# A hybrid conformer and HGRN2 block on one core: the first three chunks projected without the shift, which is added later

## The chip, the core and the metric

The kernel runs on one NeuronCore of a Trainium2 chip. Its engines are TensorE (PE, matrix products), VectorE (DVE), ScalarE (ACT), GpSimd (POOL) and SyncE (SP, which here only issues transfers). Each runs its own instructions in program order, and they wait for one another through semaphores. The metric is device time in microseconds (us) of one execution; lower is better.

## What is computed

The reference is one layer of a trunk with a sequence of 1024 tokens and a width of 1024. Only its head matters here:

```python
cond = jax.nn.silu(c)
mod = cond @ w_ada[l] + b_ada[l]
sh1, sc1, gt1, sh2, sc2, gt2 = [m[:, None, :] for m in jnp.split(mod, N_MOD, axis=-1)]
h = rms_norm(x, g_pre_mix[l]) * (1.0 + sc1) + sh1
zin = h @ w_in[l]
cv_val, cv_gate, q, f, i, og = jnp.split(zin, splits, axis=-1)
out_a = conformer_conv(cv_val, cv_gate, ...)   # u = val * sigmoid(gate), a causal convolution of 31 taps
out_b = hgrn2(q, f, i, og, lb_all[l], hgrn_norm_g[l])
...
```

`sc1` (the scale) and `sh1` (the shift) each take the product of `cond` with a 1024 x 1024 block of `w_ada`, 4 MB each. `w_in` is 1024 x 3072.

## The kernel before

Everything is float32. A product of two float32 matrices is made of three fp32r products: each operand is split into a high part (a copy rounded to fp32r) and a low part (the operand less its high part), and high x high, high x low and low x high are summed in PSUM.

The input projection is done in 24 chunks of 128 output columns, in five per head (`gate`, `val`, `i`, `f`, `q`) for four heads and then four `og` chunks. A chunk runs over 8 slices `kt` of the width, with 6 matmuls of 128x512 in each: 48 in all. Chunk g uses the PSUM pair g % 2, the weight slot g % 3 (`WS`) and the raw slot g % 2 (`RAW`). The normalised, scaled and shifted tokens, turned so that the width lies on the partitions, are `ha_hi`, `ha_lo` (kt 0 to 3) and `hb_hi`, `hb_lo` (kt 4 to 7).

**The prelude**, until the tokens are ready, works in 16 groups (`GROUPS`), each one kt and one half of the tokens. For a group PE turns four tiles of x (`turn_x`, L1989); ACT takes them out of PSUM with scale and shift at once (`full_and_high`, L994) and rounds them to the high part (L998); DVE subtracts for the low part (`low_half`, L1426), which counts `h_ready`; then PE projects the group for chunks 0 and 1 (`project_group`, L2004, six matmuls per group). Scale and shift come in four blocks of 256 columns: DVE sums 8 rows of a block, scale and shift side by side in 512 columns (`sum_rows`, L1400, L1403, L1408), PE sums over the partitions (`mod_sums`, L1976), and DVE adds the bias rows (`scale_shift`, L1415, L1417). A group cannot be turned before its block's numbers are there.

The order of work within an engine is written out by hand; nothing is scheduled by a planner. SP loads block 0, four tiles of x, the weights of chunks 0 and 1 (`load_chunk`, L541), the other four tiles of x, and blocks 1 to 3. POOL splits the weights of chunks 0 and 1 when they land, and those of chunk 2 only after `acc_ready` has reached 4, that is after DVE's last block; then it writes `masks_late` and clears `pmat`.

**The main part** is a loop over five periods of 40 pieces (a piece is one kt of one chunk; period 0 starts at piece 16, which is chunk 2). PE projects, and between projections runs small steps of the head before, called slots (`SLOTS`, `PLACES`). Slot `M` (L1953) sums the next rows of ada over the partitions; it waits until POOL has added all eight rows (`add_ada`, L756). The `S` slots are the levels of the recurrence, in which DVE does the work between. POOL's order in the first turns is: low parts of chunks 3 and 4 (`low`, L744), a row of ada, the low part of chunk 5, two rows, a late tap (L765), and so on to the rows 6 and 7. DVE does 54 steps of the convolution per head (`tap`, L1524), spread by `TAPS_FIRST` (how many of them in the head's own period) and the rest over the first 16 pieces of the next period; the first tap needs u = val * sigmoid(gate) (`gated`, L1510). `chunk_freed(1)`, for which chunk 3 waits, is the count of `gated`.

## Time and profile before

| | |
|---|---|
| time, median of 3 runs | 1127.62 us (1127.52 to 1127.94) |
| span of the profiled execution | 1124.7 us |
| between the span and the median | 2.9 us |
| PE busy | 1089.5 us, 97% of the span |
| DVE busy | 823.3 us, 73% |
| POOL busy | 751.2 us, 67% |
| ACT busy | 498.9 us, 44% |
| granted TensorE clock | 1.00 in the stretches looked at |

The profile holds one execution. Its page and the trace behind it give, for each instruction, when it ran and what ended the idle time before it. An instruction that is held up after it has been issued is shown as longer, not as waiting. The profiled execution's own time is not given apart from its span; the 2.9 us around the span are taken to stay as they are.

### The profile page before, as it was taken

The numbers are of one execution on the slowest core, as the hardware profiler recorded it, in microseconds if no ns is written. First come the engines' busy times: TensorE is split into PE (matmuls) and PEld (weight loads), VectorE is DVE, ScalarE is ACT, GpSimd is POOL, SyncE is SP. The second block draws the span as 40 slices with busy tenths as digits, with TensorE's granted clock in tenths as the row PEclk, the third lists the DMA queues.
The fourth block names the chain that finished last, engine by engine and source line by source line (L and its number), as shares of the span: only waits on it lengthen the run. The fifth ranks groups of instructions, "written<-read, shape, count | busy, mean of one in ns | idle before, by whom it ended". The sixth has DMA issues, their size and how long they took to land.

```text
span 1124.7 us, 14554 instructions
## 1 busy us (share of the span) xinstructions
PE 1089.5 (97%) x5140; PEld 907.7 (81%) x5140; DVE 823.3 (73%) x1168; ACT 498.9 (44%) x815; POOL 751.2 (67%) x645
## 2 busy tenths in 40 slices
PE   2899999999999999999999999999999999999996
PEld 1688888888888888888888888888888888888885
DVE  5977997979998755678775767666666666666658
ACT  5665575574652834345333323333333333233334
POOL 4179666675773640427977777868686969696966
PEclk9999999999999999999999999999999999999999
DMA  9644332333311271202322222222221222222217
GB/s 330 198 143 136 99 111 74 115 94 95 94 38 38 70 249 75 93 26 80 92 68 65 76 66 71 71 63 71 62 77 58 74 68 66 70 63 74 66 48 297
DMA packets 104745, 107.49 MB, mean 96 GB/s; under 512 B 6525, under 2 KB 84578, under 8 KB 104674
## 3 DMA queue, kind: packets, MB, share of 16 engines
q1 hardware_dynamic: 103216, 102.26, 29.0%
q10 hardware_dynamic: 1458, 4.31, 1.0%
q8 instruction: 41, 0.67, 0.3%
q14 instruction: 30, 0.25, 0.1%
HBM read 98.16 MB, written 8.40 MB: 95 GB/s over the span
## 4 chain that ended last, share of the span: by engine, by line
PE 94%; DVE 2%; ACT 1%; SPq 1%; issue 1%; DMA 1%; DVEq 0%; ACTq 0%
PE pair L2235 34%; PE pair L2041 23%; PE pair L2255 17%; PE pair L2144 8%; PE pair L2077 2%; PE pair L2198 2%; PE pair L2278 2%; PE pair L2004 1%; DMA x<-in_x 1%; DVE acc L1403 1%; PE pair L2072 1%; PE pair L2091 1%; PE pair L1965 1%; SPq L541 1%; PE pair L2093 1%
## 5 line engine op out<-in xcount | busy, mean ns | idle before, releaser
L1826 DVE TENSOR_TENSOR yt<-yt,pair 128x512 f32<-128x512 f32 x264 | 176.2, 684 | 34.6 <-PE pair L2255 34.6
L1524 DVE SCALAR_TENSOR_TENSOR pair<-u,conv_w_col,pair 128x512 f32<-128x512 f32 x208 | 139.6, 750 | 1.9 <-ACT pair L1120 1.4
L844 POOL TENSOR_TENSOR raw_r<-raw,w_hi 128x512 fp32r<-128x512 f32 x68 | 96.3, 1417 | 65.1 <-ACT w_hi L1256 65.1
L756 POOL TENSOR_TENSOR acc<-acc,ada 128x256 f32<-128x256 f32 x112 | 92.1, 854 | 55.9 <-ACT ada L1057 54.6
L2255 PE MATMUL pair<-w_hi,op_hi 128*128 128x512 f32 x280 | 109.2, 390 | 0.0
L2255 PE MATMUL pair<-w_hi,op_lo 128*128 128x512 f32 x280 | 109.0, 389 | 0.0
L2255 PE MATMUL pair<-w_lo,op_hi 128*128 128x512 f32 x280 | 108.9, 389 | 0.0
L853 POOL TENSOR_TENSOR w_lo<-w_lo_f,w_hi 128x512 fp32r<-128x512 f32 x70 | 95.1, 1359 | 0.0
L2235 PE MATMUL pair<-t_lo,w_hi 128*128 128x512 f32 x240 | 93.7, 390 | 0.0
L2235 PE MATMUL pair<-t_hi,w_hi 128*128 128x512 f32 x240 | 93.4, 389 | 0.0
L744 POOL TENSOR_TENSOR w_lo<-raw,w_hi 128x256 fp32r<-128x256 f32 x84 | 66.9, 828 | 23.1 <-ACT w_hi L1013 22.9
L1256 ACT ACTIVATE w_hi<-raw 128x512 fp32r<-128x512 f32 x68 | 42.7, 627 | 72.9 <-PE pair L2235 71.7
L2041 PE MATMUL pair<-ha_hi,w_hi 128*128 128x512 f32 x192 | 63.0, 409 | 0.6 <-ACT sg L1024 0.6
L2235 PE MATMUL pair<-hb_hi,w_hi 128*128 128x512 f32 x160 | 62.6, 392 | 0.0
L2235 PE MATMUL pair<-hb_lo,w_hi 128*128 128x512 f32 x160 | 62.6, 391 | 0.0
L2235 PE MATMUL pair<-ha_lo,w_hi 128*128 128x512 f32 x160 | 62.3, 390 | 0.0
L2235 PE MATMUL pair<-ha_hi,w_hi 128*128 128x512 f32 x160 | 62.2, 389 | 0.0
L2041 PE MATMUL pair<-hb_hi,w_hi 128*128 128x512 f32 x192 | 62.0, 404 | 0.0
L2255 PEld LDWEIGHTS pair<-w_lo,op_hi 128*128 128x128 f32 x280 | 52.6, 188 | 11.2
L2255 PEld LDWEIGHTS pair<-w_hi,op_lo 128*128 128x128 f32 x280 | 52.6, 188 | 11.2
L2255 PEld LDWEIGHTS pair<-w_hi,op_hi 128*128 128x128 f32 x280 | 52.6, 188 | 11.1
L2041 PE MATMUL pair<-ha_lo,w_hi 128*128 128x512 f32 x192 | 59.7, 392 | 0.0
(330 smaller groups left out, 2951.0 us busy)
## 6 DMA issues: line engine op xcount, KB each, us to landing
ada<-in_w_ada SPq DMA_DIRECT2D x48, 512.0 KB, 3.9
raw<-in_w_ffn_in SPq DMA_DIRECT2D x56, 256.0 KB, 3.0
raw<-in_w_in SPq DMA_DIRECT2D x24, 512.0 KB, 3.8
w_lo_f<-in_w_ffn_out SPq DMA_DIRECT2D x40, 256.0 KB, 3.1
w_hi_f<-in_w_ffn_out SPq DMA_DIRECT2D x30, 256.0 KB, 3.1
x<-in_x SPq DMA_DIRECT2D x8, 512.0 KB, 8.2
raw<-in_w_out SPq DMA_DIRECT2D x8, 512.0 KB, 3.4
x<-in_x SPq DMA_DIRECT2D x4, 1024.0 KB, 8.7
```

What stands on the lines that cost most here:

```text
L744: i_ = pool.tensor_tensor(w_lo[:, g % WS, cols], raw[:, g % RAW, cols], w_hi[:, g % WS, cols], ALU.subtract)
L756: i_ = pool.tensor_tensor(acc[:, cols], acc[:, cols], ada[:, n % 2, cols], ALU.add)
L844: pool.tensor_tensor(place_part(at), place_full(at), place_part(GU_HIGH[m % 3]), ALU.subtract).then_inc(gu_low, 1)
L853: pool.tensor_tensor(place_part(at), place_full(at), place_part(DOWN_HIGH[d % 2]), ALU.subtract).then_inc(down_low, 1)
L1256: act.activation(place_part(GU_HIGH[m % 3]), place_full(WEIGHT_PLACES[e][k]), ACT.Copy).then_inc(gu_high, 1)
L1524: i_ = dve.scalar_tensor_tensor(out=dst, in0=tap_of(j + 1, h), scalar=tap_weight(j + 1, t), in1=dst, op0=ALU.mult, op1=ALU.add)
L1826: i_ = dve.tensor_tensor(dst, dst, bank(4 + t), ALU.add)
L2041: i_ = pe.matmul(dst[:, cols], w, x[:, cols], start=first and s_ == 0, stop=last and s_ == 2)
L2077: i_ = pe.matmul(dst[:, cols(i)], keys[:, half % 2, cols(i)], right_queries(i, 1 << half), start=True, stop=True)
L2144: i_ = pe.matmul(dst[:, cols], x, w[:, cols], start=first and s_ == 0, stop=last and s_ == 2)
L2235: i_ = pe.matmul(dst, a[:, w], x[:, n, :], start=s in (0, 1, 3, 4) and n == 0 and s_ == 0, stop=n == 3 and s_ == 2, skip_group_check=True)
L2255: i_ = pe.matmul(bank(4 + t), x, w, start=q % 2 == 0 and s_ == 0, stop=s_ == 2, skip_group_check=True)
```

## The change

It does the following.

- ada's scale is loaded and summed without the shift (blocks of 256 columns: `scales`, `sum_rows`, `scale`). The 16 groups of the prelude carry the scale alone. Their full tile is written back over x (`first_tile`), so ACT no longer waits for a free buffer.
- The shift's rows come after the scale's: the first half of its columns by DVE (`sum_shifts`), the second by ACT, POOL and DVE together (`late_shift_row`, `add_late_shifts`, `sum_late_shifts`).
- Chunks 0, 1 and 2 are projected from the scaled tokens. What the shift adds to them is a bias for each of their columns, which PE makes from the raw weights (`first_biases`) and which goes in where they are read: into the sigmoid, into `gated_first` and into `vt`.
- While PE projects chunk 2 (`project_first`, now into `pair[3]`), ACT and DVE split the tokens again with the shift (`shifted_high`, `shifted_low`), slice by slice behind PE. Chunk 3 and the later ones use these.
- The weights of chunks 0, 1 and 2 are loaded in halves into `late_next` and `late_taps` and split by POOL in halves (`load_first`, `split_first`); chunk 2's no longer wait for `acc_ready`. `masks_late` is written first.
- POOL's low part of chunk 4 and all that follows waits for `again_ready` to reach 8.
- `TAPS_FIRST` is [30, 34, 35, 42] where it was [42, 35, 35, 42], and the 18 early taps of period 0 are 11.
- One table load of ACT moves ahead of the first square, and two (Exp, sigmoid) from behind the fourth group to behind the last.

```diff
-TAPS_FIRST = [42, 35, 35, 42]
+TAPS_FIRST = [30, 34, 35, 42]
...
-            load_block(0)
+            load_scales(0)
             for i in range(TT):
                 if i == 4:
-                    for g in range(RAW):
-                        load_chunk(g)
+                    load_first(0, 0)
+                    load_first(1, 0)
                 sp.dma_start(x0[:, i, :], x_d[:, i, :]).then_inc(x_loaded[i], 16)
-            for b in range(1, 4):
-                load_block(b)
-            for g in range(RAW, 5):
-                load_chunk(g)
-            sp.wait_ge(h_ready, 16)
+            load_scales(1)
+            load_first(0, 1)
+            load_first(1, 1)
+            load_scales(2)
+            load_scales(3)
+            load_first(2, 0)
+            load_first(2, 1)
+            load_shifts(0)
+            sp.wait_ge(acc_ready, 2)
+            load_shifts(1)
+            load_chunk(WS)
+            load_chunk(WS + 1)
+            sp.wait_ge(bias_ready, 1)
...
+            def split_first(g, q):
+                cols = slice(q * HALF, (q + 1) * HALF)
+                pool.wait_ge(first_loaded_w[2 * g + q], 16)
+                me.done(pool.tensor_copy(w_hi[:, g, cols], first_raw[g][:, cols]))
+                me.wait()
+                pool.tensor_tensor(w_lo[:, g, cols], first_raw[g][:, cols], w_hi[:, g, cols], ALU.subtract
+                                   ).then_inc(w_split if q else first_split, 1)
...
+            pool.wait_ge(again_ready, KT)
             pool.memset(pmat[:, :, :], 0.0).then_inc(p_clear, 1)
-            for g in range(N_IN):
+            for g in range(2, N_IN):
...
-                if g >= 2:
-                    act.wait_ge(h_ready, g - 1)
-                act.activation(full0[:, g % 2, :], group_bank(g), ACT.Identity, scale=gs[:, 0, kt:kt + 1],
-                               bias=mod[:, kt:kt + 1]).then_inc(full0_ready, 1)
+                act.activation(first_tile(kt, half), turns_of(group_bank(g)), ACT.Copy, scale=gs[:, 0, kt:kt + 1]
+                               ).then_inc(full0_ready, 1)
...
+            def shifted_high(kt):
+                act.wait_ge(shift_ready, kt // 4 + 1)
+                if kt < KT - 1:
+                    act.wait_ge(first_used, kt + 1)
+                else:
+                    act.wait_ge(w_used, WS)
...
+            def shifted_low(kt):
+                dve.wait_ge(again_hi, kt + 1)
+                dve.scalar_tensor_tensor(out=turns_of(lo[:, kt % 4, :]), in0=x0[:, :, kt * P:(kt + 1) * P],
+                                         scalar=mod[:, kt:kt + 1], in1=turns_of(hi[:, kt % 4, :]), op0=ALU.add,
+                                         op1=ALU.subtract).then_inc(again_ready, 1)
...
+            def first_biases():
+                pe.wait_ge(shift_ready, 2)
+                for g in range(WS):
+                    for kt in range(KT):
+                        i_ = pe.matmul(bank(4)[:, 4 + g:5 + g], first_raw[g][:, kt * P:(kt + 1) * P], mod[:, kt:kt + 1],
+                                       start=kt == 0, stop=kt == KT - 1)
+                i_.then_inc(bias_made, 1)
...
+            def project_first():
+                pe.wait_ge(w_split, WS)
+                for kt in range(KT):
+                    hi, lo = (ha_hi, ha_lo) if kt < 4 else (hb_hi, hb_lo)
+                    split_product(pair[3], 2, slice(kt * P, (kt + 1) * P), hi[:, kt % 4, :], lo[:, kt % 4, :],
+                                  kt == 0, kt == KT - 1).then_inc(first_used if kt < KT - 1 else w_used, 1)
+                    if kt == 1:
+                        shift_sums(0)
+                    if kt == 3:
+                        shift_sums(1)
+                    if kt == 5:
+                        first_biases()
...
+                    if g == WS:
+                        pe.wait_ge(again_ready, kt + 1)
```

Three places show what moves. The first is DVE behind the last group of the prelude; these are its rows before (`hb_lo` is the low part, `u` the gated value, `pair<-u` a tap):

```order
64 L1426 TENSOR_TENSOR hb_lo<-ggb,hb_hi 128x512 x4
65 L1378 RECIPROCAL lb_tmp<-lb_tmp 128x4
66 L1380 TENSOR_TENSOR lb_tmp<-lb_tmp 128x4
67 L1382 TENSOR_TENSOR lb_tmp<-lb_tmp 128x4
68 L1384 TENSOR_SCALAR one_less_lb<-lb_tmp 128x4
69 L1498 MEMSET u 128x30
70 L1510 TENSOR_TENSOR u<-sg,pair 128x512
71 L1511 TENSOR_TENSOR u<-sg,pair 128x4x128
72 L1524 SCALAR_TENSOR_TENSOR pair<-u,conv_w_col,pair 128x512 x47
```

And in the changed kernel, from the last row of the shift's first half on:

```order
64 L1514 SCALAR_TENSOR_TENSOR acc_shift<-shifts,cond,acc_shift 128x512
65 L1519 TENSOR_TENSOR acc_shift<-acc_shift 128x512
66 L1617 MEMSET u 128x30
67 L1529 TENSOR_SCALAR acc_shift<-shifts_late,cond 128x512 x2
68 L1532 SCALAR_TENSOR_TENSOR acc_shift<-shifts_late,cond,acc_shift 128x512 x2
69 L1535 TENSOR_TENSOR acc_shift<-acc_shift 128x512
70 L1538 TENSOR_TENSOR acc_shift<-acc_shift,shifts_late 128x512
71 L1552 TENSOR_TENSOR mod<-pair,vec 128x4
72 L1568 SCALAR_TENSOR_TENSOR ha_lo<-x,mod,ha_hi 128x1024
73 L1552 TENSOR_TENSOR mod<-pair,vec 128x4
74 L1568 SCALAR_TENSOR_TENSOR ha_lo<-x,mod,ha_hi 128x1024 x3
75 L1568 SCALAR_TENSOR_TENSOR hb_lo<-x,mod,hb_hi 128x1024
```

Between the last low part of the prelude and `gated`, DVE now has the end of the shift's sums and six of the eight low parts of the second split; the taps before the first slot are 40 where they were 47.

The second place is PE in chunk 2. Before, its rows are 48 matmuls of L2041 with nothing between them; now the sums of the shift and the biases (`pair<-mod,late_next` and `late_taps`, the raw weights) stand among them:

```order
129 L2238 MATMUL pair<-ha_hi,w_lo 128x512 x2
130 L2117 MATMUL pair<-ones,acc_shift 128x1 x4
131 L2238 MATMUL pair<-hb_hi,w_hi 128x512 x2
132 L2238 MATMUL pair<-hb_lo,w_hi 128x512 x2
133 L2238 MATMUL pair<-hb_hi,w_lo 128x512 x2
134 L2238 MATMUL pair<-hb_hi,w_hi 128x512 x2
135 L2238 MATMUL pair<-hb_lo,w_hi 128x512 x2
136 L2238 MATMUL pair<-hb_hi,w_lo 128x512 x2
137 L2152 MATMUL pair<-mod,late_next 128x1 x16
138 L2152 MATMUL pair<-mod,late_taps 128x1 x8
```

A first set of four sums (L2117) stands after the second slice, the second after the fourth, and 24 products of one column after the sixth.

The third place is POOL between the masks and the rows of ada. Before:

```order
27 L736 CAST w_hi<-raw 128x1024
28 L738 TENSOR_TENSOR w_lo<-raw,w_hi 128x1024
29 L736 CAST w_hi<-raw 128x1024
30 L738 TENSOR_TENSOR w_lo<-raw,w_hi 128x1024
31 L718 MEMSET masks_late 128x448
```

Now, after the masks:

```order
46 L829 CAST w_hi<-late_next 128x512
47 L831 TENSOR_TENSOR w_lo<-late_next,w_hi 128x512
48 L829 CAST w_hi<-late_taps 128x512
49 L831 TENSOR_TENSOR w_lo<-late_taps,w_hi 128x512
50 L829 CAST w_hi<-late_taps 128x512
51 L831 TENSOR_TENSOR w_lo<-late_taps,w_hi 128x512
52 L840 TENSOR_TENSOR shifts_late<-shifts_late 128x512 x3
53 L794 TENSOR_TENSOR w_lo<-raw,w_hi 128x256 x4
54 L853 MEMSET pmat 128x1024
```

Chunk 2's split (the `late_taps` rows) used to stand behind the wait for DVE's last block, and now runs when its weights land; three additions of shift rows and chunk 3's low part follow it ahead of the clearing of `pmat`.

## Rows read from the trace of the kernel before

**Rows 1.** Chain that ended last, in order of time: start us, us, what

```profile
11.98 8.48 DMA x<-in_x
...
64.60 1.03 ACT sg L1024
65.63 0.14 issue
65.77 35.62 PE pair L2041 x156
...
117.26 1.68 PE pair L1953 x16
```

**Rows 2.** Windows: stretch, length, busy us (instructions) by engine, clock, DMA share, GB/s

```profile
core 0: us, PE busy (x) PEld busy (x) DVE busy (x) ACT busy (x) POOL busy (x), PEclk, DMA share, GB/s
20.48:65.77 45.29, 36.41 (x184) 28.66 (x182) 37.05 (x71) 31.15 (x49) 15.84 (x21) 1.00 0.65 204
69.48:106.78 37.30, 37.30 (x173) 31.07 (x172) 30.13 (x46) 23.60 (x25) 30.31 (x42) 1.00 0.46 141
117.26:1110.00 992.74, 992.00 (x4677) 827.92 (x4676) 721.40 (x1000) 423.83 (x709) 675.38 (x545) 1.00 0.26 82
```

**Rows 3.** DMA rate in 40 equal slices of the first 70 us

```profile
GB/s 0 241 342 346 364 385 384 363 308 298 373 410 400 362 348 349 349 347 348 347 350 349 348 322 292 146 6 0 0 0 0 0 5 277 18 0 33 328 253 0
```

**Rows 4.** Timeline of ACT: start us, us, line, operation, count, idle before

```profile
24.34 1.06 ACT L953 ACTIVATE w_hi<-x 128x1024 fp32r<-128x1024 f32 x1
25.63 0.76 ACT L994 ACTIVATE ggb<-pair,mod,gs 128x512 f32<-128x512 f32 x1
26.43 0.63 ACT L998 ACTIVATE ha_hi<-ggb 128x512 fp32r<-128x512 f32 x1
```

**Rows 5.** Timeline of DVE, first 120 us, same columns

```profile
8.53 4.06 DVE L1403 SCALAR_TENSOR_TENSOR acc<-ada,cond,acc 128x512 f32<-128x512 f32 x6
...
29.04 0.88 DVE L1400 TENSOR_SCALAR acc<-ada,cond 128x512 f32<-128x512 f32 x2
29.88 0.69 DVE L1426 TENSOR_TENSOR ha_lo<-ggb,ha_hi 128x512 fp32r<-128x512 f32 x1
30.49 1.41 DVE L1403 SCALAR_TENSOR_TENSOR acc<-ada,cond,acc 128x512 f32<-128x512 f32 x2
...
68.56 31.05 DVE L1524 SCALAR_TENSOR_TENSOR pair<-u,conv_w_col,pair 128x512 f32<-128x512 f32 x47 [1.42 <-ACT pair L1120]
107.28 0.74 DVE L1597 COPY_PREDICATED pmat<-ident,pair 128x512 f32<-128x512 int32 x1 [7.67 <-PE pair L2072]
```

**Rows 6.** Timeline of DVE, where POOL was at work too

```profile
17.65 1.50 DVE L1389 TENSOR_SCALAR x<-x,rs 128x1024 f32<-128x1024 f32 x1
...
54.87 2.18 DVE L1426 TENSOR_TENSOR hb_lo<-ggb,hb_hi 128x512 fp32r<-128x512 f32 x1 [0.43 <-ACT hb_hi L998]
```

**Rows 7.** Timeline of POOL

```profile
17.57 1.04 POOL L736 CAST w_hi<-raw 128x1024 fp32r<-128x1024 f32 x1 [10.32 <-DMA raw<-in_w_in]
...
53.77 2.73 POOL L738 TENSOR_TENSOR w_lo<-raw,w_hi 128x1024 fp32r<-128x1024 f32 x1
...
63.48 0.95 POOL L782 MEMSET pmat<- 128x1024 f32 x1
66.65 5.65 POOL L744 TENSOR_TENSOR w_lo<-raw,w_hi 128x256 fp32r<-128x256 f32 x8 [2.21 <-ACT w_hi L1013]
72.24 2.84 POOL L756 TENSOR_TENSOR acc<-acc,ada 128x256 f32<-128x256 f32 x4
...
106.78 8.12 POOL L756 TENSOR_TENSOR acc<-acc,ada 128x256 f32<-128x256 f32 x8
```

**Rows 8.** Groups of all instructions by line and shape: busy us, mean ns, idle before

```profile
L844 POOL TENSOR_TENSOR w_lo<-w_lo_f,w_hi 128x512 fp32r<-128x512 f32 x36 | 48.0, 1335 | 15.9 <-ACT w_hi L1256 15.9
L1638 DVE SCALAR_TENSOR_TENSOR y<-pair,y 128x1024 f32<-128x1024 f32 x4 | 4.7, 1212 | 0.0
L1036 ACT ACTIVATE f<-f,lb_tmp,one_less_lb 128x1024 f32<-128x1024 f32 x4 | 5.0, 1241 | 0.0
```

**Rows 9.** Chain in order of time, the last groups of the prelude

```profile
58.78 0.44 PE pair L1989 x4
59.22 1.39 PE pair L2004 x6
```

More of the change, by code:

```diff
@@ L575, in _, with load_scales, load_shifts @@
-            load_block(0)
+            def load_scales(b):
+                for q in range(2):
+                    rows = slice(4 * q, 4 * q + 4)
+                    sp.dma_start(scales[:, b, rows, :], w_ada_d[:, rows, D + b * 2 * P:D + (b + 1) * 2 * P]
+                                 ).then_inc(scales_loaded[2 * b + q], 16)
+            def load_shifts(b):
+                dst = shifts_late if b else shifts
+                for q in range(2):
+                    rows = slice(4 * q, 4 * q + 4)
+                    sp.dma_start(dst[:, rows, :], w_ada_d[:, rows, b * HALF:(b + 1) * HALF]
+                                 ).then_inc(shifts_loaded[2 * b + q], 16)
@@ L1020, in evacuate @@
                 act.wait_ge(w_used, g + 1)
-                if kind == "gate":
-                    if t:
-                        act.wait_ge(u_evac, t)
+                if g == 0:
+                    act.wait_ge(bias_ready, 1)
+                    act.activation(sg[:, :], src, ACT.Sigmoid, bias=first_bias[:, 0:1]).then_inc(chunk_evac, 1)
+                elif kind == "gate":
+                    act.wait_ge(u_evac, t)
                     act.activation(sg[:, :], src, ACT.Sigmoid).then_inc(chunk_evac, 1)
+                elif g == 2:
+                    act.wait_ge(again_ready, KT)
+                    act.activation(vt[:, :], pair[3][:, :], ACT.Identity, bias=first_bias[:, 2:3]).then_inc(chunk_evac, 1)
                 elif kind == "i":
-                    if t:
-                        act.wait_ge(*slot_done(t - 1, 1))
+                    act.wait_ge(*slot_done(t - 1, 1))
                     act.activation(vt[:, :], src, ACT.Copy).then_inc(chunk_evac, 1)
@@ L1150, in ln_step @@
                     act.preload_act_table_set("silu_and_others")
-            act.wait_ge(h_ready, 16)
+            high(WS)
+            for kt in range(KT - 2):
+                shifted_high(kt)
             evacuate(0)
-            high(WS)
+            for kt in range(KT - 2, KT):
+                shifted_high(kt)
+            act.wait_ge(vec_ready, 3)
             for period in range(5):
@@ new lines, in sum_late_shifts @@
+            def sum_late_shifts():
+                for j in range(KT // 2, KT):
+                    dst = acc_shift[:, 1, j % 2, :]
+                    if j == KT // 2:
+                        dve.wait_ge(shifts_loaded[3], 16)
+                    if j < KT // 2 + 2:
+                        me.done(dve.tensor_scalar(dst, shifts_late[:, j, :], cond[:, j:j + 1], None, ALU.mult))
+                    else:
+                        me.wait(behind=1)
+                        me.done(dve.scalar_tensor_tensor(out=dst, in0=shifts_late[:, j, :], scalar=cond[:, j:j + 1], in1=dst,
+                                                         op0=ALU.mult, op1=ALU.add))
+                me.wait()
+                me.done(dve.tensor_tensor(acc_shift[:, 1, 0, :], acc_shift[:, 1, 0, :], acc_shift[:, 1, 1, :], ALU.add))
+                me.wait()
+                dve.wait_ge(late_shift_added, KT // 2 - 1)
+                dve.tensor_tensor(acc_shift[:, 1, 0, :], acc_shift[:, 1, 0, :], shifts_late[:, 0, :], ALU.add
+                                  ).then_inc(late_shift_summed, 1)
@@ L1437, in _ @@
                 normalise_x(i)
-            scale_shift(0)
-            scale_shift(1)
+            scale(0)
+            scale(1)
             normalise_x(4)
```

273 lines of the change are left out of this document (186 added, 87 removed).

## The prediction

> **What bounds the kernel now.** I read the chain in order of time first [rows 1]. Up to 65.77 us it goes from engine to engine (transfers of x, ACT, DVE, PE by turns); from 65.77 us it is PE alone. The windows say the same [rows 2]: from 20.48 to 65.77 us PE is busy 36.41 of 45.29 us, and behind 117.26 us 992.00 of 992.74. So the end moves with the last wait of PE that the change makes or takes away, and everything behind it moves by as much. The two dates to watch are PE's entry into chunk 3 (before: chunk 2 begins at 65.77, and 48 matmuls at 35.62/156 = 0.228 us are 10.9, so 76.7) and its slot M at 117.26 [rows 1], 40.6 us later. Of the 20.48 to 65.77 us DVE is busy 37.05, more than PE, and POOL only 15.84 [rows 2].
>
> **Prices.** DVE per instruction by spacing [rows 5]: two SBUF operands and a scalar, 128x512, 4.06/6 = 0.68; one operand, 0.84/2 = 0.42; the low part 30.49 - 29.88 = 0.61. For 1024 elements the first kind takes 1.21 [rows 8], so 512 elements are 0.53 and 256 are 0.27: a 256-wide row costs 0.41, the 256-wide addition 0.34, and the one-operand form, which is quicker per element, I estimate at 0.28. A block of scale alone is 2 x 0.28 + 6 x 0.41 + 0.34 = 3.4 us, where one of both was 2 x 0.42 + 6 x 0.68 + 0.61 = 5.5. PE's float32 products stand in the trace as two records each: M has eight products and 16 records in 1.68 us [rows 1], 0.21 each. A turn is 0.44 and a group 1.39 [rows 9].
>
> **The front.** Ahead of the last tile of x there are 1 MB less of ada and 0.5 MB less of weights. At the 350 and 300 GB/s of those stretches [rows 3] that is 3.0 + 1.8 = 4.8 us. The table load that moves ahead of the first square falls into the wait for x (the chain's 8.48 us of transfer [rows 1]) and costs nothing; without that cover it would be 1.3. So ACT's first tile comes at 25.63 - 4.8 = 20.8 [rows 4], its high part at 22.2, the first low part at 22.8.
>
> **POOL against DVE.** Here the change adds something that the old order kept apart. When POOL's CAST ran from 17.57 to 18.61, DVE's 128x1024 product took 1.50 us; when POOL subtracted until 56.50 (53.77 + 2.73), DVE's low part took 2.18 for 0.69 and ended 0.55 after POOL did [rows 6, 7]. The taps, with one operand in PSUM, keep their 0.66 while POOL runs [rows 5]. So a low part or product in SBUF and a POOL instruction go one after the other. That DVE's two-operand row sums are held up as well no row shows; their operands lie in SBUF as the low part's do, and I take them as held. The bounds are nothing and all of it.
> The Trainium skill (SBUF — State Buffer, SBUF: two separate sides) says that the pair of ports is "an exclusive lock, not a bandwidth split", for DVE instructions with two SBUF inputs against a GpSimd one that reads SBUF. The trace agrees for the low part; by that rule the row sums are held too, which is the full sum below, and by the shown rows alone it would be nearer to the half case.
> In the old prelude POOL was idle from chunk 1's split to `acc_ready` 4. Now four POOL instructions (second halves of chunks 0 and 1) land on DVE's second block, four on its third (chunk 2) and three additions on its fourth. A half split is 0.52 (half of 1.04) and 1.1 to 1.34 [rows 7, 8], say 1.8 together: 3.6, 3.6 and 3.8 us.
>
> **The prelude.** DVE from 22.8: block 1 and a low part, 4.0, with POOL 3.6: 30.4. A low part and two scales, 0.9: 31.3, and PE turns the fifth group. From there to the last low part DVE has 13 low parts (7.9), two blocks (6.8), four scales (0.5) and seven shift rows (4.2), 19.4 us; POOL takes 6.9 more (7.4, 0.5 of it beside PSUM work), and I leave 1.5 for waits on ACT: 59.1. PE's last group ends at 60.6, where ACT's sigmoid started at 64.60: 4 us won. PE alone would need, from 31.3, 12 turns, 14 groups and four sums, 25.6 us, and end at 56.9; so DVE decides, and each us of POOL's counts.
>
> **Chunk 2.** PE has 10.9 us, two sets of four sums (1.7) and 24 biases (5.0), from 60.6 to 78.2. Removed are half of the prelude's sums, 8 x 0.21 = 1.7, of which DVE's waits already held the time. The shift's chain on DVE: last row and addition, 1.3, to 60.4; the late sums 2 x 0.42 + 2 x 0.68 + 2 x 0.61 = 3.4, to 63.8; chunk 3's low part on POOL (four of 0.71, from the eight in 5.65 [rows 7]) holds them 2.8 more, 66.6. ACT's high part with a bias is at most its 1.24 [rows 8], DVE's low part 1.2: shift's second half is ready at 69.3, before PE needs it at 70.5 (60.6, four slices of 1.36, the sums, two slices). Biases to 75.5; then DVE, in order: the copy 0.2, low part 1.2, lower bounds 0.8, `gated_first` 1.3: 79.0. Chunk 3 starts at 79.0, not 76.7: **2.3 us late.** The 4 us won and the 0.8 us that PE no longer waits for the sigmoid [rows 1] are less than 6.7 of new products and 0.8 of DVE's tail behind them.
>
> **Slot M.** POOL's queue behind `again_ready` holds chunk 4's low part and every row of ada for M. The last two low parts end at 81.4 (ACT's last high part waits for PE's 78.2; DVE does them after `gated_first`). Then pmat 0.95, and the work that stood from 69.48 to 106.78, 30.31 busy [rows 2]: 112.7. The last two rows are 8 x 0.71 = 5.7 to the measured 8.12 [rows 7]: 118.4 to 120.8. PE arrives at 79.0 + 40.6 = 119.6. So M comes between 119.6 and 120.8; I take 120.2, which is 117.26 + **2.9**. ada's loads, which now wait for `bias_ready`, are asked for at 75.7 and used behind 83; hidden, up to some 4 us.
> Taps: DVE starts at 81.4, and 40 x 0.66 = 26.4 end at 107.8, before the slot that came at 107.28 [rows 5] and now at 109.6. Behind it stand seven more taps than before, 4.6 us; less the 1.8 to spare they could hold PE up to 2.8. I take nothing, since M's wait gives DVE time, and keep the 2.8 for the range.
>
> **The sum.** The span would be 1124.7 + 2.9 = 1127.6, and with the 2.9 that lie between span and median 1130.5 us. About 0.2% (2.3 us) is what a measurement of this kernel can tell from no change.
>
> **The rivals.**
> POOL's work mostly falls into DVE's waits. For it: ACT and PE have waits in the prelude, and transfers may land later than DVE gets there. Against it: DVE's own 25 us are all but contiguous. Turn at 27.7, PE alone 25.6 to 53.3, chunk 2 with its additions to 70.9, biases to 68.2, gated at 71.9, M between POOL's 111.3 to 113.7 and PE's 112.5, say 113.1: 4.2 us won, 1123.4. This ends on the other side.
> Half of it is hidden (the row sums not held): turn at 29.5, PE bound again, 55.1, chunk 2 to 72.7, gated 73.7, M at 114.9: 1125.2. With three quarters exposed the last low part is at 56.5 and M at 117.6: 1128. That is the point that decides: below it the change gains, above it each us costs one.
> The front doesn't come earlier, because the transfers ahead of x drain no sooner: nothing in [rows 3] speaks for it, 1135.
> The forecast with DVE's taps holding slots: 1133.3.
>
> **How the numbers follow.** Full exposure 0.48 (with it the taps 0.08): slower. About three quarters, 1125.4 to 1129.8: 0.19, no difference. Half or less, 1123 to 1125.3: 0.31, faster. The front not earlier 0.02, slower. The range from 1123.5 to 1133.3 leaves out a little of the fast case and the 1135; the likeliest case alone is 1129.6 to 1133.3. Faster 0.31, same 0.19, slower 0.50.
>
> **What would show it.** ACT's first tile near 20.8; DVE's low parts and row sums longer than 0.69 and 0.41 wherever POOL splits; PE's last prelude group at 60.6; 24 biases in 5.0 us; DVE's `gated_first` the releaser of chunk 3 at 79.0; POOL's last row of ada the releaser of M. Wrong it would be above all if the row sums run beside POOL at full speed, or if a PE column product costs less between projections than in M.

## The result, and the profile after

The changed kernel takes **1141.05 us** (median of 4 runs, 1139.27 to 1141.23), the kernel before 1127.57 in the same runs (1127.26 to 1127.94): a ratio of **1.0117**, 95% interval 1.0103 to 1.0132. Forecast were 1130.5 us in a range from 1123.5 to 1133.3. The sign was right, the size was not: 13.5 us slower instead of 2.9. The profiled execution's span is 1136.0 us, 11.3 more than before. It was the fastest of the four (1139.27 us; the spans of the others are 1137.9 to 1139.1), so the trace accounts for 11.3 of the 13.5 us; the rest has no trace.

The windows of the changed kernel cover the front and prelude, chunk 2, chunk 3 to slot M, the stretch behind M, and one stretch of the last period (columns as in [rows 2]).

```profile
core 0: us, PE busy (x) PEld busy (x) DVE busy (x) ACT busy (x) POOL busy (x), PEclk, DMA share, GB/s
20.48:61.55 41.07, 34.48 (x164) 26.58 (x165) 37.32 (x66) 27.20 (x43) 13.90 (x11) 1.00 0.67 212
61.55:82.96 21.41, 21.41 (x113) 18.94 (x113) 14.52 (x21) 9.27 (x9) 4.49 (x4) 0.84 0.16 50
82.96:126.83 43.87, 40.40 (x194) 33.61 (x194) 41.60 (x59) 32.43 (x33) 39.78 (x50) 0.99 0.47 144
126.83:133.00 6.17, 6.17 (x27) 5.98 (x28) 0.84 (x3) 1.15 (x1) 5.05 (x6) 0.50 0.27 87
...
300.00:350.00 50.00, 49.33 (x284) 42.87 (x284) 48.78 (x75) 31.09 (x56) 35.63 (x38) 1.00 0.21 64
```

The prelude is 4.2 us shorter than before (chunk 2 begins at 61.55, before at 65.77, [rows 1]). Chunk 2 then takes 21.4 us, where the kernel before took 10.9. Two of the stretches have a granted clock well below 1.00: 0.84 in chunk 2, and 0.50 (that is 1.2 GHz, the lower of the two levels) behind M. The 0.99 ahead of M is the same fall: the clock is at 0.50 from 126.3 us on, while PE still waits. The timeline of PE shows what stood in these stretches.

```profile
71.00 0.62 PE L2238 MATMUL pair<-hb_hi,w_lo 128*128 128x512 f32 x2
71.46 3.63 PE L2152 MATMUL pair<-mod,late_next 128*128 128x1 f32 x32
74.95 3.38 PE L2152 MATMUL pair<-mod,late_taps 128*128 128x1 f32 x16
78.20 1.20 PE L2238 MATMUL pair<-hb_hi,w_hi 128*128 128x512 f32 x2
79.20 1.05 PE L2238 MATMUL pair<-hb_lo,w_hi 128*128 128x512 f32 x2
...
82.32 0.63 PE L2238 MATMUL pair<-hb_hi,w_lo 128*128 128x512 f32 x2
82.79 0.62 PE L2238 MATMUL pair<-ha_hi,w_hi 128*128 128x512 f32 x2
...
122.74 0.61 PE L2238 MATMUL pair<-ha_hi,w_lo 128*128 128x512 f32 x2
126.83 3.54 PE L2117 MATMUL pair<-ones,acc 128*128 128x1 f32 x16 [3.48 <-POOL acc L806]
130.24 2.05 PE L2288 MATMUL pair<-qk,keys 128*128 128x128 f32 x8
131.94 1.20 PE L2238 MATMUL pair<-ha_hi,w_hi 128*128 128x512 f32 x2
```

The 24 bias products are 48 records from 71.46 to 78.20, 6.7 us. The last eight of the 24 take as long as the first sixteen, and the pair of slice matmuls behind them takes 1.05 us instead of 0.62. So chunk 3 begins at 82.8. The second loss is at slot M: PE stands idle for 3.5 us and waits for POOL's last row of ada; then M takes 3.54 us and the S behind it 2.05. The same two in PE's timeline of the kernel before:

```profile
117.10 1.84 PE L1953 MATMUL pair<-ones,acc 128*128 128x1 f32 x16
118.80 1.15 PE L2077 MATMUL pair<-qk,keys 128*128 128x128 f32 x8
```

POOL's timeline in the changed kernel tells why it was late.

```profile
85.58 0.95 POOL L853 MEMSET pmat<- 128x1024 f32 x1 [18.98 <-DVE hb_lo L1568]
86.50 2.84 POOL L794 TENSOR_TENSOR w_lo<-raw,w_hi 128x256 fp32r<-128x256 f32 x4
...
95.95 5.80 POOL L806 TENSOR_TENSOR acc<-acc,ada 128x256 f32<-128x256 f32 x8 [1.04 <-ACT ada L1147]
...
115.24 4.81 POOL L794 TENSOR_TENSOR w_lo<-raw,w_hi 128x256 fp32r<-128x256 f32 x4
120.02 6.67 POOL L806 TENSOR_TENSOR acc<-acc,ada 128x256 f32<-128x256 f32 x8
```

It stood idle for 19 us until DVE had made the eighth low part of the second split (`again_ready` 8). Then it worked without a pause but one of 1.04, in which ACT waited for a transfer of ada; in SP's order that transfer stands behind chunk 6's raw load.

For the comparisons below, one landmark serves: PE's first VT slot of a period. In the kernel before the first stands at 101.22 and the second at 173.46, 72.2 us on. In the changed kernel they stand at 107.29 and 186.34, 6.1 and 12.9 later. Of this 12.9 the last period gives back some: at 300 to 350 us the granted clock is 1.00 for 0.97 before, 1.5 us. (The kernel before is at 0.50 from 332.0 to 335.4 us, which the stretch of [rows 2] from 117.26 to 1110 us averages out.)

A landmark is not exact. No experiment changes anything ahead of DVE's first low part, and yet it begins between 22.2 and 23.2 us in the traces of the changed kernel and of 1 to 12 and 14 (23.06 in the changed kernel). So up to 1 us of a difference between two kernels' landmarks need not come from an edit; where it matters, times are counted from that low part.

### The profile page after: what moved, and what is told of

It reads as the page before. It is cut to its first block, busy times and chain, and to the rows that moved or that the text cites. A ratio compares the mean times of both kernels' runs of the same rounds, so it can differ in the third digit from the quotient of the medians.

```text
span 1136.0 us, 14685 instructions
## 1 busy us (share of the span) xinstructions
PE 1100.5 (97%) x5188; PEld 917.1 (81%) x5188; DVE 838.2 (74%) x1186; ACT 507.8 (45%) x827; POOL 756.6 (67%) x654
## 4 chain that ended last, share of the span: by engine, by line
PE 90%; POOL 3%; DVE 3%; issue 1%; DMA 1%; ACT 1%; SPq 0%; DVEq 0%; POOLq 0%; ACTq 0%
PE pair L2451 34%; PE pair L2238 19%; PE pair L2471 17%; PE pair L2360 8%; PE pair L2288 2%; PE pair L2414 2%; PE pair L2494 2%; POOL acc L806 1%; DMA x<-in_x 1%; POOL w_lo L794 1%; PE pair L2182 1%; PE pair L2117 1%; DVE acc_scale L1496 1%; PE pair L2302 1%; PE pair L2129 1%
## 5 line engine op out<-in xcount | busy, mean ns | idle before, releaser
L806 POOL TENSOR_TENSOR acc<-acc,ada 128x256 f32<-128x256 f32 x112 | 89.5, 830 | 58.8 <-ACT ada L1147 57.5
L794 POOL TENSOR_TENSOR w_lo<-raw,w_hi 128x256 fp32r<-128x256 f32 x84 | 69.3, 855 | 21.5 <-ACT w_hi L1099 21.4
L2451 PE MATMUL pair<-hb_lo,w_hi 128*128 128x512 f32 x160 | 62.4, 390 | 0.0
L2451 PE MATMUL pair<-ha_lo,w_hi 128*128 128x512 f32 x160 | 62.4, 390 | 0.0
L2471 PEld LDWEIGHTS pair<-w_lo,op_hi 128*128 128x128 f32 x280 | 52.6, 188 | 11.3
L2471 PEld LDWEIGHTS pair<-w_hi,op_lo 128*128 128x128 f32 x280 | 52.5, 188 | 10.9
L2238 PE MATMUL pair<-hb_lo,w_hi 128*128 128x512 f32 x192 | 60.0, 394 | 0.0
```

What stands on the lines that cost most here:

```text
L794: i_ = pool.tensor_tensor(w_lo[:, g % WS, cols], raw[:, g % RAW, cols], w_hi[:, g % WS, cols], ALU.subtract)
L806: i_ = pool.tensor_tensor(acc[:, cols], acc[:, cols], ada[:, n % 2, cols], ALU.add)
L2238: i_ = pe.matmul(dst[:, cols], w, x[:, cols], start=first and s_ == 0, stop=last and s_ == 2)
L2451: i_ = pe.matmul(dst, a[:, w], x[:, n, :], start=s in (0, 1, 3, 4) and n == 0 and s_ == 0, stop=n == 3 and s_ == 2, skip_group_check=True)
L2471: i_ = pe.matmul(bank(4 + t), x, w, start=q % 2 == 0 and s_ == 0, stop=s_ == 2, skip_group_check=True)
```

## The experiments

Each edit is against the changed kernel unless said. "First VT" and "second VT" are the landmarks.

| kernel | time, us | ratio to before (95%) | first VT | second VT |
|---|---|---|---|---|
| changed | 1141.05 | 1.0117 (1.0103 to 1.0132) | 107.29 | 186.34 |
| 1: three bias products | 1133.69 | 1.0047 (1.0032 to 1.0063) | 101.80 | 180.46 |
| 2: chunk 4's split early | 1135.45 | 1.0067 (1.0052 to 1.0082) | 105.30 | 182.15 |
| 3: biases in three eights | 1137.49 | 1.0087 (1.0070 to 1.0104) | 103.90 | 183.10 |
| 4: M and an S later | 1139.91 | 1.0103 (1.0085 to 1.0122) | 107.83 | 182.63 |
| 5: M alone later | 1133.97 | 1.0054 (1.0037 to 1.0071) | 106.86 | 179.17 |
| 6: additions on DVE | 1140.72 | 1.0111 (1.0096 to 1.0127) | 109.74 | 188.60 |
| 7: 2, 3, 5 and 6 together | 1133.08 | 1.0046 (1.0031 to 1.0061) | 102.33 | 178.47 |
| 8: chunk 2's split late | 1144.00 | 1.0145 (1.0125 to 1.0165) | 109.65 | 189.93 |
| 9: second halves later | 1141.42 | 1.0120 (1.0102 to 1.0138) | 108.14 | 187.43 |
| 10: 7, lower bounds ordered | 1129.73 | 1.0023 (1.0013 to 1.0033) | 102.24 | 174.58 |
| 11: 10 and 9 | 1129.41 | 1.0019 (1.0009 to 1.0030) | 102.32 | 174.66 |
| 12: 11, last places | 1126.96 | 0.9999 (0.9990 to 1.0009) | 102.09 | 174.42 |
| 13: before, last places | 1124.93 | 0.9979 (0.9971 to 0.9988) | 101.28 | 173.53 |
| 14: 12 without 9, chunk 2's split at sum 4 | 1129.30 | 1.0010 (1.0001 to 1.0019) | 103.83 | 176.21 |

### The bias products and the clock

**Experiment 1.**

```diff
-                    for kt in range(KT):
+                    for kt in range(1):
```

> Only the first of each chunk's eight one-column bias products is made (3 of 24); the rest of the shift's part in the first three chunks is left out. The changed kernel's 24 took 6.71 us, the two slices behind them 4.63 where two slices are 2.7 at the full clock. Theory A (products and the clock that they lower hold chunk 3, and POOL's queue to slot M hangs on the same moment, by the last low parts): 5.9 us fewer products, 1.9 of the slices back, less about 1 because DVE's gated_first, which ends 3.3 us behind the biases, becomes the releaser: chunk 3 at 76 us for 82.96, POOL's last row 7 us earlier, M's wait unchanged near 3.5 us, time 1134. Rival B (the products cost only their 5.0 us, the clock fell for another reason): 4.4 us, 1136.7. Rival C (POOL's queue to M does not hang on the biases): M stays at 126.8, time 1141.

Measured 1133.69, theory A's number (this kernel leaves out most of the shift's part in the first three chunks and serves only to price the products). Chunk 3 begins at 77.22, 5.6 us earlier, and the granted clock from 61.5 to 78.4 us is 1.00. PE now stands idle for 2.05 us ahead of chunk 3. The profile names no releaser for it, but `gated_first` ends at 77.12, just ahead of it: once the products are gone, that is what chunk 3 waits for.

**Experiment 3.** The copy of the biases is cut in two as well.

```diff
-                    if kt == 5:
-                        first_biases()
+                    if kt >= 4 and kt < KT - 1:
+                        first_biases(kt - 4)
```

> The 24 bias products stand in three eights behind the fifth, sixth and seventh slice of chunk 2 instead of in one piece behind the sixth. Theory A (it is the unbroken 6.7 us of one-column products that lowers the clock): the granted clock of 65 to 84 us comes back to 1.00, the products take 5.0 us and the slices 1.36 each, chunk 3 at 79.4 for 82.96; POOL's queue to M starts as much earlier; time 1137.4. Rival B (each one-column product costs 0.28 us wherever it stands, the clock stays down): 1141. Rival C (the last eight delay the second split or DVE): 1142.

Measured 1137.49: theory A to a tenth. This is the third kernel's timeline of PE over the three eights and the start of chunk 3.

```profile
69.88 1.84 PE L2154 MATMUL pair<-mod,late_next 128*128 128x1 f32 x16
71.58 0.71 PE L2240 MATMUL pair<-hb_hi,w_hi 128*128 128x512 f32 x2
...
73.05 1.84 PE L2154 MATMUL pair<-mod,late_next 128*128 128x1 f32 x16
...
76.23 1.84 PE L2154 MATMUL pair<-mod,late_taps 128*128 128x1 f32 x16
...
79.40 0.62 PE L2240 MATMUL pair<-ha_hi,w_hi 128*128 128x512 f32 x2
```

The same 48 records, never slower than 1.84 us for 16, and the matmuls between them stay at 0.62. So the products themselves cost near what was forecast (3 x 1.84 with the overlaps of the records, near 5.4 us for 5.0), and of the 3.4 us by which chunk 3 comes earlier 3.2 were the lower clock that came with 24 of them in one piece (chunk 2 had begun 0.2 earlier here).

### Slot M

**Experiment 2.**

```diff
             low(WS)
+            low(WS + 1)
             pool.wait_ge(again_ready, KT)
...
             high(WS)
+            high(WS + 1)
             for kt in range(KT - 2):
```

> Chunk 4's split (ACT's high part, POOL's low part of 2.84 us) stands right behind chunk 3's, ahead of POOL's wait for again_ready, so that chunk 6's raw load is asked for sooner too and ada's third row no longer waits behind it (1.0 us). Theory A (slot M waits for POOL's queue behind again_ready, and the 3.5 us in which PE stands idle there cost another 2.8 us at a lower clock behind it): POOL's last row at 122.8 for 126.65, which is ahead of PE's 123.5, no wait, no lower clock, time 1135.0. Rival B (the lower clock behind M does not come from the wait): 3.3 us, 1137.8. Rival C (the low part holds DVE's shifted low parts, chunk 3 comes later by up to 2.8): 1138.

Measured 1135.45, near theory A, but not by its steps alone: the wait is shorter, not gone, and the lower clock came all the same. These are the second kernel's PE timeline at M and its windows around.

```profile
122.46 2.29 PE L2119 MATMUL pair<-ones,acc 128*128 128x1 f32 x16 [1.09 <-POOL acc L806]
124.61 2.05 PE L2290 MATMUL pair<-qk,keys 128*128 128x128 f32 x8
```

```profile
117.00:123.00 6.00, 4.91 (x26) 3.86 (x25) 6.00 (x11) 4.02 (x5) 5.86 (x8) 1.00 0.42 129
123.00:129.00 6.00, 6.00 (x27) 5.45 (x27) 3.84 (x8) 1.15 (x1) 4.98 (x6) 0.57 0.28 89
```

From first to second VT are 76.85 us, 4.6 over the 72.2 of the kernel before, for a wait of 1.09 us: 3.5 us are the lower clock behind it. The expected sum was reached because chunk 3 came earlier than expected too (80.8 for 82.8): 0.4 us of it the start of chunk 2, and 1.6 a lower clock that lasted for a shorter time in this run (76.5 to 79.8 us, where the changed kernel has it from 75.2 to 81.9). The edit changes nothing of what PE does there, so this part of the gain counts as luck.

**Experiment 4.**

```diff
-PLACES = [1, 1, 4, 4, 7, 10, 10, 13,
+PLACES = [1, 1, 4, 4, 7, 13, 13, 13,
```

> Slot M and the S behind it stand three pieces later in every period. PE would come to M at 123.5 + 3 x 1.36 = 127.6, behind POOL's 126.65. Theory A (the wait and the lower clock behind it are what M costs): 3.5 + 2.8 us come back, time 1135. Rival B (the lower clock behind M does not come from the wait): 1137.8. Rival C (three slots in one piece, or the later sums, make PE wait for DVE's keys or masks): 1139 or more.

Rival C in the end, but its trace says most about the clock: M stands behind no wait, and the S behind the next slice behind one of a microsecond, on DVE's qk.

```profile
127.80 1.84 PE L2117 MATMUL pair<-ones,acc 128*128 128x1 f32 x16
129.50 1.15 PE L2288 MATMUL pair<-qk,keys 128*128 128x128 f32 x8
131.69 2.05 PE L2288 MATMUL pair<-qk,keys 128*128 128x128 f32 x8 [1.03 <-DVE qk L1719]
133.39 1.20 PE L2238 MATMUL pair<-hb_hi,w_hi 128*128 128x512 f32 x2
```

The same S form takes 1.15 us without a wait and 2.05 with one. M's one-column products, behind no wait, run at the full clock (1.84 us). The next two periods repeat it: at the same S PE waits 0.90 us for ACT's keys, and the S takes 2.04 and 2.00 us.

**Experiment 5.** M alone goes back, behind the S that followed it; the keys' table is adapted.

```diff
-SLOTS = ["VT", "VT", "DIAG", "DIAG", "S", "M"] + ["S"] * 6
+SLOTS = ["VT", "VT", "DIAG", "DIAG", "S", "S", "M"] + ["S"] * 5
-PLACES = [1, 1, 4, 4, 7, 10, 10, 13,
+PLACES = [1, 1, 4, 4, 7, 10, 12, 13,
```

> Slot M alone stands later, behind the S that followed it and two pieces on (piece 12 for 10); the S stay where they were. PE would come to M at 123.5 + 0.8 + 2 x 1.36 = 127.0, behind POOL's 126.65. Theory A (M's wait and the lower clock behind it cost 3.5 + 2.8 us): no wait of a us in 115 to 135 us, granted clock 1.00 there, time 1135. Rival B (the one-column products of M lower the clock by themselves): M takes 3.5 us again behind no wait, 1137.8. Rival C (the wait goes to the next S, since DVE's or ACT's work for it comes no sooner): a wait near 1 us with the lower clock behind it, 1138 to 1140, as where the S stood later too.

Measured 1133.97, a little under theory A. No wait in the period, M at 1.84, 72.31 us from VT to VT. This kernel's M has a cost of its own in the last period: there PE now waits 1.45 us for pmat at M, where the changed kernel waited 0.67 at an S, and the clock of 300 to 350 us is 0.97 again.

### POOL beside DVE in the prelude

**Experiment 6.**

```diff
-            add_late_shifts()
             low(WS)
...
             def sum_late_shifts():
+                for j in range(1, KT // 2):
+                    dve.wait_ge(late_shift_product, j + 1)
+                    if j > 1:
+                        me.wait()
+                    me.done(dve.tensor_tensor(shifts_late[:, 0, :], shifts_late[:, 0, :], shifts_late[:, j, :], ALU.add))
```

> The three additions of the late shift rows are DVE's, behind the last low part, instead of POOL's beside the last low parts. Theory A (DVE and POOL exclude each other, DVE decides the end of the prelude): the two low parts of 1.77 and 1.75 us at 55 to 58 take 0.69, the last prelude group ends at 59.4 for 61.55; chunk 3's low part on POOL holds the now longer late sums, by 1 us more than PE has to spare at the most; M's wait stays; time 1139. Rival B (PE decided the end of the prelude already): last group at 61.5, 1141. Rival C (the late sums now come too late for the second sums of shift, PE waits there 1 us or more and then runs at the lower clock): the gain is lost, 1141 or more.

Theory A's step and rival C's price. Without POOL beside them the low parts take 0.69 us, and the prelude's last matmul is at 59.15 for 61.16, 2.0 us earlier. Of this 0.9 is an earlier start (first low part at 22.18 for 23.06). Between traces with the same clock the edit is worth 1.6: from DVE's first low part to PE's last matmul of the prelude 7 and 10, which have this edit, need 36.5 us, and the changed kernel, 2 and 5 need 38.1, all with a clock of 1.00 at 28 to 37 us. (The sixth itself needs 37.0, with 0.81 there.) Then PE waits 1.0 us for the late sums, and the gain goes. Timeline of PE in the sixth kernel:

```profile
65.34 0.61 PE L2241 MATMUL pair<-ha_hi,w_lo 128*128 128x512 f32 x2
66.97 1.05 PE L2120 MATMUL pair<-ones,acc_shift 128*128 128x1 f32 x8 [1.01 <-DVE acc_shift L1541]
67.89 0.71 PE L2241 MATMUL pair<-hb_hi,w_hi 128*128 128x512 f32 x2
68.43 0.90 PE L2241 MATMUL pair<-hb_lo,w_hi 128*128 128x512 f32 x2
69.13 1.05 PE L2241 MATMUL pair<-hb_hi,w_lo 128*128 128x512 f32 x2
...
76.13 3.55 PE L2155 MATMUL pair<-mod,late_taps 128*128 128x1 f32 x16
...
83.95 1.06 PE L2241 MATMUL pair<-hb_hi,w_lo 128*128 128x512 f32 x2
```

Here the lower clock is seen to arrive among matmuls of one form: 0.71, 0.90, 1.05, about 1.5 us behind the end of the wait, in the midst of dense work.

**Experiment 8.** `split_first(2, q)` stands behind a wait for `h_ready` 16 and behind the late additions, instead of behind `ss_ready`.

> POOL splits chunk 2 behind the last low part (h_ready 16), where its instructions meet no low part and no row sum of the prelude. Theory A (each us of POOL's beside the row sums and low parts holds DVE as long): DVE's stretch from 31 to 60 is 3.6 us shorter, the last low part at 56.1 for 59.7 and the last prelude group at 58.0; but PE then waits for the split until 60.5 and the late sums are held 3.6 us: no gain in time, 1141 to 1143. Rival B (row sums run beside POOL unheld, the long low parts only take up DVE's own waits): last low part at 59 or later, 1144.

Measured 1144.0. The exclusion of the row sums is plain, in DVE's timeline of the changed kernel (first fence) and of the eighth (second):

```profile
33.41 1.62 DVE L1561 TENSOR_TENSOR ha_lo<-x,ha_hi 128x512 fp32r<-128x512 f32 x1
34.95 2.66 DVE L1496 SCALAR_TENSOR_TENSOR acc_scale<-scales,cond,acc_scale 128x256 f32<-128x256 f32 x3
...
41.36 1.27 DVE L1496 SCALAR_TENSOR_TENSOR acc_scale<-scales,cond,acc_scale 128x256 f32<-128x256 f32 x3
```

```profile
33.42 0.69 DVE L1561 TENSOR_TENSOR ha_lo<-x,ha_hi 128x512 fp32r<-128x512 f32 x1 [0.42 <-ACT ha_hi L1068]
34.03 1.27 DVE L1496 SCALAR_TENSOR_TENSOR acc_scale<-scales,cond,acc_scale 128x256 f32<-128x256 f32 x3
...
41.36 1.27 DVE L1496 SCALAR_TENSOR_TENSOR acc_scale<-scales,cond,acc_scale 128x256 f32<-128x256 f32 x3
```

Without POOL the low part and the three rows are 2.3 us shorter, and yet DVE is back at the same place at 41.36. It waits for ACT, which waits for PE; and PE had the lower clock from 32 to 36 us in this run (1.00 in the changed kernel's). The last low part came at 59.5 for 59.0: rival B by its number, though its reason (row sums unheld) is excluded. The 0.5 us are the clock: 1, 3 and 4, whose prelude is the changed kernel's, had the lower clock at this place too, and need 38.6 us from the first low part to the prelude's last matmul, for 38.1 without it. The eighth needs 38.6 as well. So at that clock moving chunk 2's split out of the prelude won nothing: what POOL held there fell into waits of DVE's. Whether it would win something at the full clock no run shows.

**Experiment 9.**

```diff
-            for q in range(2):
-                for g in range(2):
-                    split_first(g, q)
-            pool.wait_ge(ss_ready, TT)
+            for g in range(2):
+                split_first(g, 0)
+            pool.wait_ge(acc_ready, 2)
+            for g in range(2):
+                split_first(g, 1)
```

> POOL splits the second halves of chunks 0 and 1 behind the second sum of rows (acc_ready 2) instead of beside it; chunk 2's split follows as before. Theory A (the exclusion costs time where PE waits for DVE, which is at 27 to 31 us and at 55 to 58, and nothing in between, where PE is the busy one): DVE's low part at 25.35 takes 0.69 for 1.76, its four rows 1.66 for 3.05, PE turns the fifth group at 28.9 for 31.33, and the end of the prelude comes 1.4 to 2.4 us earlier (59.2 to 60.2); M's wait stays; time 1139. Rival B (each us of POOL's counts wherever it stands): the 3.6 us only move, prelude's end 61.5, 1141. Rival C (PE, now ahead, falls to the lower clock at 32 us as in two runs here): 1140.5.

Measured 1141.42: rival B. PE turns the fifth group at 28.09 for 31.33, but then, in the ninth kernel's timeline of PE:

```profile
33.41 0.50 PE L2183 MATMUL pair<-ha_hi,w_hi 128*128 128x512 f32 x1 [1.01 <-DVE ha_lo L1562]
...
37.60 0.50 PE L2183 MATMUL pair<-ha_hi,w_hi 128*128 128x512 f32 x1 [2.09 <-DVE ha_lo L1562]
```

The changed kernel waited 0.79 in this stretch. Of 3.2 us only 0.8 reached the end of the prelude (60.6 for 61.4), and 0.4 of these are an earlier start (first low part at 22.64 for 23.06). Chunk 2's lower clock, longer here (73.8 to 83.6 us), took them and more: chunk 3 begins at 83.5 for 82.8. Within the prelude the waits only moved.

**Experiment 14** asks the same with chunk 2's split behind `acc_ready` 4, in the repaired kernel (below).

> The kernel with all edits and the last period's places, but chunks 0 and 1 split as in the change, and chunk 2's split behind the fourth sum of rows (acc_ready 4), where the kernel before had it. Theory A (where PE stands ready, each us in which POOL holds DVE delays it, as moving the halves showed: the waits only moved): PE's wait of 0.8 us at 38 us goes, DVE at 46 to 50 us has slack for the 3.6 us, the prelude's end comes 0.8 us earlier, at 58.3, time 1126.2. Rival B (the split only moves its cost to 46 to 50 us): 1127. Rival C (the low parts behind 46 us now come late for PE and it costs more there): 1128 or more.

Measured 1129.3, with runs from 1126.2 to 1130.1. The wait of 0.8 us at 38 us is gone, a longer one has come at 49.5 us, and the profiled execution has a clock of 0.76 at 32 to 37 us.

```profile
49.48 0.50 PE L2187 MATMUL pair<-hb_hi,w_hi 128*128 128x512 f32 x1 [1.20 <-DVE hb_lo L1568]
```

This is rival C, by its number (1128 or more) and by its reason: from the first low part to the prelude's last matmul this kernel needs 38.4 us, where the sixth, with the same additions on DVE, the same lower clock and the split in its early place, needs 37.0. The wide spread of the runs goes with the clock: the granted clock over the whole run is 0.997 to 0.998 in the three fastest (1126.2 to 1127.4) and 0.995 or 0.996 in all above 1129. Where it falls only the one trace shows.

### The repairs together

**Experiment 7** has 2, 3, 6 (with both low parts behind the late sums), M alone one piece later, and DVE's sixth second low part and the lower bounds behind `gated_first`.

> Together: chunk 4's split ahead of again_ready (with chunk 3's behind the late sums), the biases in three eights, the additions on DVE, M alone one piece later and behind the S, and DVE's sixth second low part and the lower bounds behind gated_first. Theory A (the four costs found are the whole loss, and they add): last prelude group at 59.4, chunk 3 at 77.3 for the 76.7 of the kernel before, no wait at M, no lower clock: the span 0.6 us over that of before, time 1128.3, a tie. Rival B (one cost comes back elsewhere, as the late sums held by POOL or DVE behind gated_first): 1130 to 1133. Rival C (the front's 4 us count fully): 1126.

Measured 1133.08: rival B. Chunk 3 began at 77.72, near the 77.3 forecast, but PE waited 1.95 us at M: ACT's first tap had waited 3.4 us for the lower bounds, which I had put too late, and with it ACT's rows and POOL's.

**Experiment 10** puts the lower bounds ahead of the last three low parts.

> The kernel with all four edits, with the lower bounds ahead of the last three second low parts again (ACT's first tap had waited 3.4 us for them, and POOL's rows of ada behind it). Theory A (M's wait of 1.9 us and the lower clock behind it came from that order): POOL's last row at 119.4 for 122.5, ahead of PE's 120.7, no wait, full clock; the period's start 72.3 us behind 102.3, 3.9 us won: time 1129.2. Rival B (ada's transfers or the held low part keep POOL at 122): 1133.

Measured 1129.73: theory A. The second VT moved from 178.47 to 174.58, 3.9 us for a wait of 1.95: half of it was the clock.

**Experiment 11** adds experiment 9.

> The same with the second halves of chunks 0 and 1 split behind the second sum of rows. Theory A (their 2.4 us at 25 to 31 are the only exposed part of POOL's early splits, and all behind moves by as much): chunk 3 at 75.3 to 76.3, time 1127.3, as the kernel before. Rival B (they only move): 1129.2. Rival C (the late sums or gated_first are now late for PE): 1129 or more.

Measured 1129.41: rival B, as in 9 (rival C names nearly the same time, but chunk 3 came no later).

**Experiment 12** is about the last period, and 13 gives the same edit to the kernel before.

```diff
-PLACES_LAST = [0, 0, 3, 3, 5, 7, 7, 9, 11, 13, 15, 17, 19, 19, 21, 21, 24, 25, 30, 31]
+PLACES_LAST = [0, 0, 3, 3, 5, 8, 8, 10, 12, 14, 16, 18, 20, 20, 22, 22, 24, 25, 30, 31]
```

> The same, and in the last period the second S, M and the S behind stand one piece later (the places 7, 7, 9 to 17, 19, 19, 21, 21 become 8, 8, 10 to 18, 20, 20, 22, 22). Theory A (PE's wait of 1.4 us for pmat there, 0.7 in the kernel before, and the lower clock behind it cost 2 to 3 us): no wait, granted clock 1.00 at 300 to 350 us, time 1124.8, 0.25% under the kernel before. Rival B (the wait moves to a later slot of that period): 1127.3.

> The kernel before, with the last period's places moved by one as in the twelfth kernel and nothing else. Theory A (the 2.4 us that those places gave there belong to them alone, not to the change): PE's 0.69 us wait for pmat at 332 us and the lower clock behind it go, time 1127.6 - 2.2 = 1125.4, so that the repaired change is still 1 to 2 us behind the kernel before where both have the same places. Rival B (in the kernel before M stands ahead of the second S and covers most of it): 1127.

1126.96 and 1124.93. The twelfth has theory A's step (no such wait, clock 1.00 at 300 to 350 us) and its gain, 2.5 us on the eleventh; its time is nearer to rival B's only because the eleventh had not reached the 1127.3 that theory A counted from. The thirteenth is theory A. Window 300 to 350 us of the kernel before, and of the thirteenth:

```profile
300.00:350.00 50.00, 49.30 (x275) 42.95 (x274) 47.05 (x72) 28.28 (x54) 32.68 (x34) 0.97 0.17 54
```

```profile
300.00:350.00 50.00, 50.00 (x282) 42.94 (x281) 47.53 (x73) 28.27 (x54) 35.50 (x37) 1.00 0.17 54
```

A wait of 0.69 us is gone and with it the lower clock behind it. With equal places the repaired change stays behind the kernel before: 12 at 0.9999 (0.9990 to 1.0009) against 13 at 0.9979 (0.9971 to 0.9988). **The thirteenth kernel, the old prelude with other places in the last period, is 0.2% faster than the kernel before, and faster than every form of the change that was tried.**

## Why the prediction was wrong

**The front, right but for 0.9 us.** ACT's first tile was forecast at 20.8 and came at 21.7, and the first low part ended at 23.7 for 22.8. DVE's work up to the fifth turn then took 1 us less than my sum: 31.33 for 31.3.

**POOL against DVE: the hold right, its price not.** Row sums are held as low parts are (0.89 us each for 0.42 at 34.95). What the Trainium skill says of an exclusive lock (SBUF — State Buffer, SBUF: two separate sides) agrees with these traces for DVE instructions with two SBUF operands (these rows, and the low part at 33.41 with 1.62 for 0.69). But "DVE decides, and each us of POOL's counts" did not hold. Taking the three additions away from the low parts brought the prelude's end 1.6 us forward, for 3.8 in the sum (experiments 7 and 10); moving chunk 2's split out of it won nothing, for 3.6 (experiment 8, at the lower clock); moving the second halves won 0.3, for 3.6 (experiment 9, which put them beside DVE's next rows). PE was nearer to deciding than forecast: from 31.33 us to chunk 2 it was busy for 27.1 us, not 25.6, and idle for 2.9. That chunk 2 began only 0.9 us later than the 60.6 forecast is therefore in part luck: holds that cost less made up for waits and matmuls that cost more.

**Chunk 2, the first step that failed: "24 biases (5.0)" and the two slices behind them at 1.36 each.** I priced both at the full clock. They took 6.7 and 4.6 us (for 5.0 and 2.7), of which experiment 3 gave 3.2 us back by the order alone. Chunk 3 came at 82.8 for 79.0; `gated_first`, at 81.7, was not its releaser.

**Slot M, the second: "M at 120.2".** The mechanism held: POOL's last row was the releaser. But its start hung on `again_ready`, so chunk 2's delay came a second time, into POOL's queue (85.5 for 81.4), and "hidden, up to some 4 us" was wrong for ada: its third row waited for its transfer and cost POOL 1.0. Chunk 7's low part took 4.8 us for 2.8, while DVE's qk product (128x1024, two SBUF operands) ran from 114.3 to 116.4; that the one held the other is read from the times alone. POOL was done at 126.7 for 118.4 to 120.8; PE would have arrived at 123.4 for 119.6.

**Behind M, the third, which I had not written down:** that a wait costs more than its length. M and S took 5.5 us for 2.7 at 117.26 to 119.95. The forecast's 2.9, 6.6 for M's later date (126.83 for 120.2) and 2.8 of clock make the 12.3 us by which PE leaves the S later; the slices behind it add 0.5, and 1.5 us are given back in the last period, where PE this time kept its clock. That is the 11.3 us of the span. The sign, forecast at 0.50, came out by a margin that the forecast did not contain.

The rival of the taps held by their slots did not come to pass: DVE had its 40 taps done at 112.6, 0.75 us ahead of the first diagonal's product.

## What to carry to other kernels

Where PE waits just ahead of narrow products (column sums, 128-wide slots), price the wait at its length and 1.5 to 3.5 us more (from first to second VT, less the 72.2 us of the kernel before and less the wait, 1.5 in 4, 2.0 in 7, 3.3 to 3.5 in the changed kernel, 1, 2, 3, 6 and 9, and 4.7 in 8). Here moving the slot out of reach of a late producer won more (experiment 5, 7 us) than making the producer faster (experiment 2, 5.6, of which 2 were not its doing). Long runs of tiny products belong between dense ones: the same 24 in three eights saved 3.2 us. And where one date sets two queues off, as the end of chunk 2 does PE's chunk 3 and POOL's rows, an error in it is to be carried down both.
